# First attention of a two-block network: the last unit of the query projection split over the first four turnings, first scores moved ahead of the third unit, and two quads' scaling moved from GpSimd to VectorE

## The reference, cut to what matters

```
h = rmsnorm(x, attn_pre_g)
proj = h @ w_in                       # queries, keys, values, gates
k_cmp, v_cmp = compress_kv(...)       # 31 compressed positions for each of 2 groups
gates = sigmoid(g_n)                  # (tokens, 8 heads, 3 branches)
# NSA: 8 heads in 2 groups; with N_SEL=16 >= the 8 blocks there are, the "selected"
# branch is full causal attention, and so is the window branch (window 512)
o = gates[0]*o_cmp + gates[1]*o_sel + gates[2]*o_win
# SWA: 8 heads in 2 groups, window 128, with a sink in the softmax's denominator
prob = exp(s - m) / (sum(exp(s - m)) + exp(sink - m))
mix = concat([o_nsa, o_swa]) @ w_o
```

## Time and profile before

| | us |
|---|---|
| three runs | 1607.81, 1615.59, 1617.1 |
| their median | 1615.59 |
| the profiled execution | 1611.04 |
| its span in the trace | 1609.7 |
| TensorE busy in the span | 1505.7 |

### The profile page before, as it was taken

How to read it: one execution, slowest core, us unless ns; L and a number is a source line. 1 busy time by engine, 2 the same in 40 slices (tenths; PEclk the granted TensorE clock), 3 DMA queues, 4 the chain that set the end, 5 groups by cost and what they waited for, 6 DMA issues and landing times.

```text
span 1609.7 us, 22505 instructions
## 1 busy us (share of the span) xinstructions
PE 1505.7 (94%) x8093; PEld 1283.0 (80%) x8093; DVE 1098.9 (68%) x2300; ACT 615.7 (38%) x1536; POOL 763.0 (47%) x740
## 2 busy tenths in 40 slices
PE   5998798999999999999999999999998999999997
PEld 4787555888788887887888889888986787899886
DVE  7646453566777767748867767777777488777764
ACT  3313575232122210124544554555445355344431
POOL 5856354366776649685434124413434214524430
PEclk9997799999999999999999999999998999999999
DMA  6622000333444436553311011101112321211221
GB/s 188 194 83 94 12 1 24 134 113 118 151 136 132 139 121 209 176 179 111 115 53 53 14 40 54 44 10 53 53 33 73 138 85 53 67 40 40 66 92 53
DMA packets 115886, 142.60 MB, mean 89 GB/s; under 512 B 11048, under 2 KB 75200, under 8 KB 115776
## 3 DMA queue, kind: packets, MB, share of 16 engines
q1 hardware_dynamic: 89968, 91.77, 18.3%
q10 hardware_dynamic: 25808, 49.40, 9.2%
HBM read 132.74 MB, written 8.40 MB: 88 GB/s over the span
## 4 chain that ended last, share of the span: by engine, by line
PE 66%; DVE 14%; ACT 8%; POOL 6%; issue 4%; DMA 1%; ACTq 0%; SPq 0%; DVEq 0%; POOLq 0%
PE ps L528 18%; PE ps L530 17%; PE ps L529 17%; POOL w_lo L517 3%; PE ps L1310 2%; POOL w_hi L515 2%; PE ps L1506 2%; PE ps L968 2%; PE ps L944 1%; DVE st L2940 1%; ACT p L2150 1%; PE ps L1002 1%; ACT p L1774 1%; PE ps L1520 1%; DVE newton L2398 1%
## 5 line engine op out<-in xcount | busy, mean ns | idle before, releaser
L515 POOL TENSOR_SCALAR w_hi<-w_raw 128x512 fp32r<-128x512 f32 x308 | 235.8, 766 | 636.4 <-PE ps L530 479.3
L517 POOL TENSOR_TENSOR w_lo<-w_raw,w_hi 128x512 fp32r<-128x512 f32 x316 | 442.5, 1401 | 30.2 <-ACT w_hi L1696 4.5
L528 PE MATMUL ps<-w_hi,h_hi 128*128 128x384 f32 (+2 forms) x768 | 277.9, 362 | 7.9 <-POOL w_lo L517 3.6
L530 PE MATMUL ps<-w_hi,h_lo 128*128 128x384 f32 (+2 forms) x768 | 265.7, 346 | 0.0
L529 PE MATMUL ps<-w_lo,h_hi 128*128 128x384 f32 (+2 forms) x768 | 265.2, 345 | 0.0
L528 PE MATMUL ps<-h_hi,w_hi 128*128 128x512 f32 (+1 forms) x616 | 244.2, 396 | 7.7 <-POOL w_lo L517 3.9
L530 PE MATMUL ps<-h_hi,w_lo 128*128 128x512 f32 (+1 forms) x616 | 237.3, 385 | 0.0
L529 PE MATMUL ps<-h_lo,w_hi 128*128 128x512 f32 (+1 forms) x616 | 237.1, 385 | 0.0
L2658 DVE SCALAR_TENSOR_TENSOR mod_acc<-mod_piece,csil,mod_acc 128x512 f32<-128x512 f32 x140 | 157.3, 1163 | 18.0 <-DMA mod_piece<-in_ada_w 13.9
L528 PEld LDWEIGHTS ps<-w_hi,h_hi 128*128 128x128 f32 x768 | 146.6, 191 | 20.2 <-POOL w_lo L517 5.1
L530 PEld LDWEIGHTS ps<-w_hi,h_lo 128*128 128x128 f32 x768 | 146.2, 190 | 9.3
(11 more groups left out here) (340 smaller groups left out, 3001.6 us busy)
## 6 DMA issues: line engine op xcount, KB each, us to landing
mod_piece<-in_ada_w ACTq DMA_DIRECT2D x96, 256.0 KB, 3.0
w_raw<-in_w_gate_up SPq DMA_DIRECT2D x88, 256.0 KB, 3.1
w_raw<-in_a_w_in SPq DMA_DIRECT2D x128, 128.0 KB, 2.2
w_raw<-in_w_down SPq DMA_DIRECT2D x22, 512.0 KB, 4.3
w_raw<-in_b_w_in SPq DMA_DIRECT2D x20, 512.0 KB, 3.6
w_raw<-in_w_out SPq DMA_DIRECT2D x16, 512.0 KB, 3.9
w_raw<-in_w_in SPq DMA_DIRECT2D x8, 512.0 KB, 4.1
w_raw<-in_w_o SPq DMA_DIRECT2D x8, 512.0 KB, 3.8
```

The lines of the kernel that those rows point to most:

```text
L515: pool.tensor_scalar(hi[:, e, :], raw[:, e, :], 1.0, 0.0, ALU.mult, ALU.add).then_inc(*s["pool_step"].up())
L517: m = pool.tensor_tensor(lo[:, e, :], raw[:, e, :], hi[:, e, :], ALU.subtract)
L528: pe.matmul(out, a[0], b[0], start=start, stop=False)
L530: return pe.matmul(out, a[1], b[0], start=False, stop=stop)
```

## The change

Four things are changed, all in the first attention.

1. The 16 score matmuls of quads 0 and 1 are issued by TensorE ahead of unit 2 instead of behind unit 3. Their wait is now for the low part of unit 1 (whose banks they use) and for the zeroed keys.
2. Unit 3 is no longer projected in one piece. `pe_last_queries` is a generator that issues two of its eight chunks (6 matmuls) after each of the turnings 0 to 3. It goes to bank 7 instead of bank 3 (`query_bank`), so `pe_quads` first waits for `cmp_exped` of group 1, besides the low part of unit 2.
3. ScalarE makes unit 3's high parts behind its copy of turning 4, and VectorE makes the low parts at the head of the iteration of quad 2. The scores of the SWA quad of group 1 (quad 5) wait for them. On VectorE both compressed scalings follow unit 2 and the least of group 1 directly.
4. `POOL_SCALES_FROM` is 8 and is compared with the number of the quad: quads 6 and 7 are scaled by VectorE, GpSimd begins with quad 8.

```diff
-POOL_SCALES_FROM = 1
+POOL_SCALES_FROM = 8
+LAST_QUERIES_AT = 4
+
+def query_bank(kind, j):
+    return j + 4 if kind == 0 else 7 if j == 3 else j
...
-    for j in range(4):
+    for j in range(3):
...
-        if j == 3:
-            pe.wait_ge(*s["ck_lo"].at("ck"))
-            pe.wait_ge(*s["ck_hi"].at("cv"))
+        if j == 2:
+            for slot in slots_behind(quads(), -1):
+                pe_slot_scores(k, pe, quads(), slot)
         pe_cols(k, pe, k.h1, ("q", 1), KD, j, j * P, ("q", 1, j))
...
 def pe_slot_scores(k, pe, qs, slot):
     s, q = k.sig, quad_of(qs, slot)
+    if slot == 0:
+        pe.wait_ge(*s["q_lo"].at((1, 1, 1)))
+        pe.wait_ge(*s["pool_step"].at("k_zero"))
+    if slot == [x for x in qs if x.t == 0 and x.kind == 2 and x.g == 1][0].slots[0]:
+        pe.wait_ge(*s["q_lo"].at((1, 3, 1)))
...
+def pe_last_queries(k, pe):
+    for c in range(KD):
+        if c % 2 == 0:
+            pe.wait_ge(*split_at(k, ("q", 1), c))
+        m = three(pe, k.ps[:, query_bank(1, 3), :], k.hl(("q", 1), c, 3 * P, P), [x[:, c, :] for x in k.h1], c == 0, c == KD - 1)
+        if c == KD - 1:
+            m.then_inc(*k.sig["prod"].up(("q", 1, 3)))
+        yield
...
 def pe_quads(k, pe):
-    for j in range(4):
-        pe.wait_ge(*s["q_lo"].at((1, j, 1)))
-    pe.wait_ge(*s["pool_step"].at("k_zero"))
-    for slot in slots_behind(qs, -1):
-        pe_slot_scores(k, pe, qs, slot)
+    pe.wait_ge(*s["q_lo"].at((1, 2, 1)))
+    pe.wait_ge(*s["ck_lo"].at("ck"))
+    pe.wait_ge(*s["ck_hi"].at("cv"))
+    pe.wait_ge(*s["cmp_exped"].at(1))
+    held = pe_last_queries(k, pe)
...
+            if turn_number(qs, q.n, i) < LAST_QUERIES_AT:
+                for _ in range(KD // LAST_QUERIES_AT):
+                    next(held)
...
             act_quad_copy(k, act, qs, q, i)
+            if turn_number(qs, q.n, i) == LAST_QUERIES_AT:
+                act_queries(k, act, 1, 3)
...
-    if q.t >= POOL_SCALES_FROM:
+    if q.n >= POOL_SCALES_FROM:
         dve.reciprocal(f[:, 3, :], total).then_inc(*s["b_total"].up(q.n))
...
     for q in qs:
+        if LAST_QUERIES_AT in range(turn_number(qs, q.n, 0), turn_number(qs, q.n, len(q.chunks))):
+            dve_queries(k, dve, 1, 3)
         scaled = dve_quad_scale(k, dve, qs, qs[q.n + 1]) if q.n + 1 < len(qs) else iter(())
```

More of the change, by code:

```diff
@@ L489, in pool_program @@
                     for quad in quads():
-                        if quad.t >= POOL_SCALES_FROM:
+                        if quad.n >= POOL_SCALES_FROM:
                             pool_quad_scale(k, pool, quad)
@@ L933, in pe_quad_turn @@
     if what == "keys":
-        pe.wait_ge(*s["b_scaled_p" if q.t >= POOL_SCALES_FROM else "b_scaled"].at(q.n))
+        pe.wait_ge(*s["b_scaled_p" if q.n >= POOL_SCALES_FROM else "b_scaled"].at(q.n))
     if n >= 2:
@@ L1723, in act_block_one_attention @@
     act.activation(k.hid[:, 1, :, :], k.hid[:, 2, :, :], ACT.Tanh, scale=GELU_C).then_inc(*s["hid_th"].up("hid"))
[L1725 to L1730, removed]
     for j in range(4):
-        queries(0, j)
+        act_queries(k, act, 0, j)
         if j == 0:
@@ L1744, in act_block_one_attention @@
             act.copy(k.cv[0:NCMP, :, :], k.ps[0:NCMP, 3, 64:64 + GROUPS * HD].rearrange("p (g n) -> p g n", g=GROUPS)).then_inc(*s["ck_hi"].up("cv"))
-    for j in range(4):
-        queries(1, j)
+    for j in range(3):
+        act_queries(k, act, 1, j)
         if j == 0:
@@ L1750, in act_block_one_attention, with act_queries @@
                 act.copy(k.pc[:, g, :], k.ps[:, 6 + g, :]).then_inc(*s["cmp_exped"].up(("copied", g)))
-        if j >= 2:
-            act_compressed_exp(k, act, j - 2)
+    for g in range(GROUPS):
+        act_compressed_exp(k, act, g)
     act_quads(k, act)
+def act_queries(k, act, kind, j):
+    s = k.sig
+    act.wait_ge(*s["prod"].at(("q", kind, j)))
+    for e in range(2):
+        top, head = slice(0, HD) if kind == 0 else slice(HD, P), 8 * kind + 2 * j + e
+        act.activation(k.qst[top, head, :], k.ps[e * HD:(e + 1) * HD, query_bank(kind, j), :], ACT.Copy,
+                       scale=Q_SCALES[head]).then_inc(*s["q_hi"].up((kind, j, e)))
 def act_compressed_exp(k, act, g):
@@ L2500, in dve_block_one_attention @@
     dve.tensor_scalar(k.hid[:, 0, :, :], k.hid[:, 2, :, :], 0.5, None, ALU.mult).then_inc(*s["hid"].up("hid"))
[L2502 to L2508, removed]
     for j in range(4):
-        queries(0, j)
+        dve_queries(k, dve, 0, j)
         if j == 0:
@@ L2520, in dve_block_one_attention, with dve_queries @@
             dve.tensor_tensor(k.cklo[0:HD, :, CMP_AT:CMP_AT + NCMP], src, k.ckhh[0:HD, :, CMP_AT:CMP_AT + NCMP], ALU.subtract).then_inc(*s["ck_lo"].up("ck"))
-    for j in range(4):
-        queries(1, j)
+    for j in range(3):
+        dve_queries(k, dve, 1, j)
         if 1 <= j <= 2:
             dve_compressed_least(k, dve, j - 1)
-        if j >= 2:
-            dve_compressed_scale(k, dve, j - 2)
+    for g in range(GROUPS):
+        dve_compressed_scale(k, dve, g)
     dve_quads(k, dve)
+def dve_queries(k, dve, kind, j):
+    s = k.sig
+    for e in range(2):
+        top, other = (slice(0, HD), slice(HD, P)) if kind == 0 else (slice(HD, P), slice(0, HD))
+        head = 8 * kind + 2 * j + e
+        dve.wait_ge(*s["q_hi"].at((kind, j, e)))
+        dve.scalar_tensor_tensor(k.qst[other, head, :], k.ps[e * HD:(e + 1) * HD, query_bank(kind, j), :], Q_SCALES[head],
+                                 k.qst[top, head, :], ALU.mult, ALU.subtract).then_inc(*s["q_lo"].up((kind, j, e)))
 def dve_compressed_least(k, dve, g):
```

## The result

The changed kernel took 1626.61 us, median of five runs (1623.31 to 1627.87), against 1608.33, median of five runs of the kernel before (1607.81 to 1617.1): a ratio of 1.0075, 95% interval 1.0051 to 1.0098. The quotient of the two medians is larger, 1.011, because three of the five runs of the kernel before lie near 1608 and two near 1616. The prediction, 1615.0 in 1605 to 1622, was too low.

What follows compares the result with a forecast made beforehand. VectorE's queue, not TensorE, was taken to bound the first attention's start. Delays of 1.2 - 0.6 + 0.9 gave +1.5 us on the profiled 1611.0, 1612.5; the forecast median was 1615.0, between that and the median 1615.6 plus scatter, range 1605 to 1622.

Steps and rivals of the forecast that it cites:

- Steps 1 to 4: First attention up to turning 4: first scores 133.1, first least 148.9, first key turning 153.0, turning 4 at 160.3 against 160.12.
- step 4: Held unit's four parts on TensorE: idle from 140.5 to about 146.9, full clock back during first two, turning 4 at 160.3.
- rival (b): TensorE between turnings 1 and 4: clock stays down through all four parts, +5 us, 1620; chance 0.18.
- Rival (a): TensorE is what counts: the unit fills its waits and the half clock up to 175 goes, 1607 to 1611; chance 0.28.
- signs that the forecast named for being wrong: First least before 147, or the stage ending over 2 us earlier.
- Step 5: Unit 3's low part on VectorE at quad 2's head: first scaling ends 164.1, quad 4's scores 1.2 us later.
- Step 6: Quads 3 to 5: full clock gains about 1.1 us a turn, scalings beside splitting lose about 0.9; 0.6 us back.
- Rival (c): Each VectorE scaling beside the splitting waits out a whole GpSimd instruction: twelve times 0.7, about +8 us, 1623; chance 0.03.
- Step 7: Quads 6 and 7 scaled on VectorE at 0.4 us a scaling: 0.9 us later together, bounds 0.6 and 2.4.
- The sum: Whole stage: 1.2 - 0.6 + 0.9 = +1.5 us, on the profiled 1611.0.
- Step 2: VectorE's queue to the first least: 1.3 us of slowing by GpSimd's splitting goes, yet least comes at 148.9 against 148.40.
- step 3: First scaling on VectorE: four scalings at 0.28 each with GpSimd quiet, 1.2 us less, first key turning at 153.0.

Runs made afterwards that it cites:

- a_split_late_from6: Changed kernel with GpSimd's output-weight splitting moved ahead of quads 10, 12, 16, 21, and GpSimd scaling from the seventh quad: 1616.3 us, ratio 1.0001 to the kernel before.
- a_all_three: Changed kernel with output-weight splitting moved into later gaps, GpSimd scaling from the seventh quad, unit 3's low part at quad 3's head: 1615.0 us, ratio 0.9990.
- a_split_late: Changed kernel with only GpSimd's output-weight splitting moved, in four parts ahead of quads 10, 12, 16, 21: 1620.6 us, ratio 1.0034 to the kernel before.
- a_low_late: Changed kernel with only unit 3's low part on VectorE moved from the head of quad 2 to quad 3: 1621.5 us, ratio 1.0032 to the kernel before.

## Why the prediction was wrong

- **Steps 1 to 4** came as forecast: first scores 132.52 (133.1), first least 148.25 (148.9), scalings of 0.28, turning 1 at 152.30 (153.0), clock at 1.00 in 155 to 161, turning 4 at 159.95 (160.3). TensorE's idle time of 6.42 us ahead of turning 0 is the one named in step 4. So rival (b) was wrong: the clock did not stay down through the four parts. Rival (a) was right in that it rose, and wrong in that TensorE's waits would go; they went to the turnings 5 and 6. None of the signs that the forecast named for being wrong appeared, since they looked for an earlier least or a shorter stage only.
- **Step 5**: VectorE's first scaling of quad 3 ended at 164.27 (164.1) and the scores of quad 4 were taken at 164.28, 1.4 us later (1.2). It waited 4.06 us for the held unit, and quad 3's reciprocal, the next thing that turning 5 needs, came 3.05 us later, which the step left out by comparing the scores of quad 4 alone. Quad 3's last three scalings stand behind those scores in both kernels, so against the kernel before the place costs 1.4 us there. But the place costs more than that shows: with the splitting out of the way, the low part one quad later brought quad 7 3.1 us sooner (a_split_late_from6 against a_all_three, both counted from quad 0).
- **Step 6 is the step that failed.** It put 0.25 us on each of 3 or 4 scalings a turn, against 1.1 gained: 0.6 us back over three turns. Up to quad 5's first scaling the operations beside the splitting, five groups of scalings and three sums, cost 5.9 us more than alone: 0.46 + 0.43 + 1.31 + 0.43 + 0.89 + 0.22 + 1.41 + 0.75, for 0.80, 0.59, 2.17, 0.59, 1.18, 0.38, 2.08 and 1.04 against 0.34, 0.16, 0.86, 0.16, 0.29, 0.16, 0.67 and 0.29. And the gain of the full clock went: 5.89 us of idle time ahead of turning 5, then 0.50 to 179. Turning 7 came at 179.40 against 174.61; counted from the stage's start that is +5.2, where steps 5 and 6 had +0.6. The mistake was the unit. The 0.31 us of the earlier trace rows is (2.35 - 1.12) / 4, but the 1.23 us was one wait, since that group of four ended at 153.63 and this instruction of GpSimd in the kernel before at 153.55:

```profile
152.19 1.36 POOL L517 TENSOR_TENSOR w_lo<-w_raw,w_hi 128x512 fp32r<-128x512 f32 x1
```

The mean over four was a matter of the group's size. The cost goes by groups, up to one low part each and once a little more (1.41), and there were more groups, and more of them of one scaling, in the new place. Taking the overlap away gave back 3.1 us up to quad 7, not 5.9; where the rest of the excess went, no run shows.
- The Trainium skill had it: page "SBUF — State Buffer", section "Who interferes with whom", has the two engines hold their shared port as an exclusive lock, the other blocked for the whole instruction. The runs agree: the ends fall together to 0.1 us, and an operation that met instructions of 2.3 us took up to 2.13. I took a mean from one group of rows over that rule.
- **Rival (c)** named the mechanism and its 1623 lay near the result, but in part by luck: it counted twelve waits of 0.7 by scalings, there were eight of 0.22 to 1.41, three of them by sums, and of the 11.6 us between 1626.6 and the forecast only 5.9 lie in this stage. Its chance of 0.03 was the worst number of the text.
- **Step 7** was too small as well: 0.9 us expected, within bounds of 0.6 and 2.4; from quad 6 to quad 10 it was 1.9 on the kernel before, 2.1 in the changed one and 2.3 with the splitting moved. The scalings took 0.41 as forecast; where the rest of the time goes, no run takes apart.
- **The sum** was +1.5; the stage measured +7.4. With 5.2 for 0.6 and 2.1 for 0.9 it comes to 7.3. What a reader could not see in the forecast: the kernel before paid the same lock, 6.4 us with what followed from it, and the change moved it rather than removed it. Step 2 and step 3 booked 2.5 us for its going. The order costs about 7 us even with no overlap in either kernel; the moved scores, which steps 1 and 2 had at half a microsecond, are the dearer half of it.
- **The base** was a little low: the forecast of 1615.0 less its sum of 1.5 is 1613.5, and the kernel before has medians of 1615.2 to 1616.3. The scatter of single executions goes with the clock: beside a_split_late the kernel before took 1608.1 at a mean granted clock of 0.976 and 1619.9 at 0.964. Stretches at half clock lie in stages that no edit touches too. Between 490 and 505 us, for one, before and then after:

```profile
490.00:505.00 15.00, 15.00 (x68) 12.42 (x67) 12.09 (x14) 3.82 (x6) 11.34 (x11) 1.00 0.44 130
```

```profile
490.00:505.00 15.00, 12.98 (x52) 10.70 (x51) 8.94 (x13) 3.06 (x5) 4.74 (x5) 0.77 0.27 87
```

## What to carry to other kernels

When a block of GpSimd work is moved, look at which VectorE work it comes to lie beside: each group of scalings can wait for one whole GpSimd instruction, so ask how long these are and how many groups meet them, not what a scaling takes on the mean. Before an order is redone for a wait, try to take that overlap away: four stretches of 3.9 us put into idle gaps gave 6.4 us, where the reorder lost 7.4. Behind the reorder the same edit gave 0.5, so the value of a cure is that of its place and order, and it is measured in the kernel it is meant for. A unit of matmuls that fills TensorE's wait is not free if an engine that works in a fixed order must fetch its result in the middle of the chain: here that place cost 3.1 us by quad 7.

## What was not expected of the hardware

- In the overlap of the changed kernel VectorE paid nearly alone: GpSimd's low parts kept 1.26 to 1.36 us. In the kernel before GpSimd paid twice, where it started while a VectorE product of two SBUF operands was running (142.76 and 147.31): a high part took 1.16 us instead of 0.62 (142.77), and a low part at 147.91 took 1.58.
- Not every VectorE operation waits. Leasts, from PSUM, kept 0.36 us beside the splitting, and the low parts of queries, from PSUM and one operand in SBUF, 1.41 for two (168.88 in a_low_late); scalings from SBUF to SBUF and sums of two SBUF operands waited.
- A stretch of thin work of 3.1 us (1.25 us idle and 16 short matmuls), with TensorE full ahead of it and behind it, was followed by a window at 0.50 to 0.61 in five of ten profiles. Why in these and not in the others stays open.
